# Convolution module of a flow-matching backbone: output, LayerNorm and residual in token order, mean and scale read from PSUM, relayout on two DMA queues

## The chip, the cores and the metric

The kernel runs on the 8 cores of one Trainium2 chip. All cores run the same program on different tokens and don't exchange data. The metric is the device time of the slowest core in microseconds; less is better.

## What is computed

One inference step of a backbone of four layers. Layers 0 and 2 mix tokens by neighbourhood attention, layers 1 and 3 by a convolution module; each is followed by a squared-ReLU MLP. The model width is 1024, and each core holds 1536 tokens. Only the convolution module changes:

```python
def conv_module(h, w_pw1, w_dw, b_dw, ln_g, ln_b, w_pw2):
    a, g = jnp.split(h @ w_pw1, 2, axis=-1)
    u = a * jax.nn.sigmoid(g)
    u = lax.conv_general_dilated(u, w_dw[:, None, :], window_strides=(1,),
        padding=[(15, 15)], dimension_numbers=('NWC', 'WIO', 'NWC'),
        feature_group_count=D_MODEL) + b_dw
    u = jax.nn.silu(layer_norm(u, ln_g, ln_b))
    return u @ w_pw2
# in the layer:  x = x + g1 * conv_module(modulate(rms_norm(x, norm_g), sh1, sc1), ...)
#                x = x + g2 * sq_relu_mlp(modulate(rms_norm(x, norm_g'), sh2, sc2), ...)
```

The convolution has 31 taps along the tokens and acts on each channel alone; the LayerNorm is over the 1024 channels of a token.

## The kernel before

Activations lie with channels on the partitions: 8 chunks of 128 channels by 1536 tokens, in 3 token tiles of 512 (`xT` is the f32 residual, `hT` the bf16 input of a product). The order of all work is written out by hand: a small class keeps one list per engine and puts a wait in front of an operation for each event that it needs, so each engine works its list in order. TensorE's writes go to 8 PSUM banks taken in turn; banks in `held` are left out of the turn. Weights come in 1 MB pieces by DMA on POOL's queue into a ring of three slots; `done_piece` queues the next piece, which waits until TensorE has left the slot. Small work is queued beside products: `defer` holds an operation back for some ticks, `bq` is a list of items, and `tick(n)`, called after each product, takes n of them.

`conv_layer` runs in this order:

- For each of 4 pieces of pw1 (`j`), for each token tile, four products; `pw1_evac` forms a x sigmoid(g) (ScalarE, VectorE) and writes bf16 with the tokens split by their remainder modulo 4: token = 4 tau + f, stored as f planes of tau.
- `relayout(j)` moves that piece into the convolution's layout with 16 DMAs between places in SBUF (4 channel groups q by 4 values of f), all on SP's queue.
- From the second piece on, each pw1 piece is followed by two convolution chunks of 128 channels (`conv_chunk`), and the last two (6 and 7) come after all pieces. Chunks 6 and 7 need `relayout(3)`, the last. A chunk has 4 outputs f; each is 32 matmuls into one bank of 384 columns (tau), at 4 places of the array at once. ScalarE evacuates each with the bias (L1245) into `vv`, ordered chunk, f, tau. After f = 1 and f = 3, VectorE casts the finished pair of planes to bf16 (L1253) and ScalarE squares it (L1256).
- `stats` sums channels and their squares with a matrix of ones (L1217) into banks SMB and SQB; that of chunk c stands in TensorE's list behind the first f of chunk c + 1.
- `build_w` makes a tap table (VectorE, L1198), four for each chunk; those of chunks 6 and 7 are made as soon as the chunks before have left the buffers.
- From the sums, 96 partitions wide, come mean and 1/std (L1323 to L1336). `ln_bcast(t)` spreads both over 128 partitions into two PSUM banks, and ScalarE copies them to SBUF (L1350, L1352).
- `ln_chunk(t, ch)` subtracts the mean and multiplies by the scale, two operations of 128x512 in f32 (L1366, L1370): chunks 2, 5 and 7 of every tile on POOL, the others on VectorE, each with two tiles of its own for the result. All read the SBUF copies. `ln_silu` (ScalarE, L1378) writes `hT`.
- pw2: for tile 0 the first four outputs are summed chunk by chunk while the silus arrive (L1398); then their gates, then the other products, each followed by `gate` (VectorE, L1413: residual plus gated product) and by the squares and sums of the next RMS norm (L575 on ScalarE, L582 on TensorE, L594 and L597 for its scale, L611 on VectorE, L632 on ScalarE). LayerNorm of tiles 1 and 2 and the norm of the tiles that are done are taken from `bq`, two items behind each product.

Since pw2's input is in the order f, tau, its output is so too, and `gate` reads and writes the residual, which is in token order, with a step of four elements. After `conv_layer` comes the MLP, whose products (L654) need the normed tile.

Of the kernel before, what the change touches and what calls it, by code (L numbers as in the profile page):

```python
# [347 lines left out]
def build_program():  # L348
# [763 lines left out]
    def conv_layer(l):  # L1112
# [4 lines left out]
        vv = vv.rearrange("p (c f t) -> p c f t", c=8, f=4)  # L1117
# [19 lines left out]
        for n in range(2):  # L1137
# [3 lines left out]
            up2.append((ap.rearrange("p (g w) -> p g w", g=8), parts, P.new_sem(f"cvs{l}_{n}")))  # L1141
# [29 lines left out]
        def relayout(j):  # L1171
# [11 lines left out]
            for q in range(4):  # L1183
                for f in range(4):
                    P.dma("sp", lambda e, q=q, f=f: e.dma_start(
                        out=dst[32 * f:32 * f + 32, q::4, :],
                        in_=u3[32 * q:32 * q + 32, :, f, :]),
                        dsem, reads=flat + halo, writes=[dst_r[q * 4 + f]])
# [21 lines left out]
        def stats(ch):  # L1210
            for half, bk in ((0, SMB), (1, SQB)):
                src = sqc[:, half * 1536:(half + 1) * 1536].rearrange("p (f t) -> p f t", f=4)

                def fn(e, src=src, bk=bk):
                    ins = None
                    for t in range(NT):
                        ins = e.matmul(ps[bk][32 * t:32 * t + 32, :],  # L1217
                                       lhsT=ones_b[:, 0:32], rhs=src[:, :, t * 128:(t + 1) * 128],
# [4 lines left out]
        def conv_chunk(ch):  # L1223
# [4 lines left out]
            for f in range(4):  # L1228
# [14 lines left out]
                if f == 0 and lag:  # L1243
                    stats(lag.pop(0))
                P.op("act", lambda e, f=f, pi=pi: e.activation(  # L1245
                    out=vv[:, ch, f, :], in_=ps[pi][:, 0:NTAU], func=AF.Identity,
                    bias=V("bdw", 1, i * 8 + ch)),
                    reads=[ps_r[pi], vecs_r], writes=[v_r[ch][f]])
                if f % 2 == 0:
                    continue  # L1250
                hf = f // 2
                o = hf * 768
                P.op("dve", lambda e, f=f, o=o: e.tensor_copy(  # L1253
                    out=sqc[:, o:o + 768].rearrange("p (f t) -> p f t", f=2), in_=vv[:, ch, f - 1:f + 1, :]),
                    reads=v_r[ch][f - 1:f + 1], writes=[sq_r[0][hf]])
                P.op("act", lambda e, f=f, o=o: e.activation(  # L1256
                    out=sqc[:, 1536 + o:2304 + o].rearrange("p (f t) -> p f t", f=2),
                    in_=vv[:, ch, f - 1:f + 1, :], func=AF.Square),
                    reads=v_r[ch][f - 1:f + 1], writes=[sq_r[1][hf]])
# [82 lines left out]
        def ln_bcast(t):  # L1342
            pm, pq = LB[t]
            for pb_, src, src_r in ((pm, mean, mean_r), (pq, rstd, rstd_r)):
# [6 lines left out]
                 reads=[ps_r[pm]], writes=[cm[1]])  # L1351
            P.op("act", lambda e: e.activation(out=cr[0][:, :], in_=ps[pq][:, :], func=AF.Copy),  # L1352
                 reads=[ps_r[pq]], writes=[cr[1]])

        def ln_chunk(t, ch):
            tc = slice(t * 128, (t + 1) * 128)
            (m_, m_r), (r_, r_r) = cpy[t % 2]
            if ch in (2, 5, 7):
# [187 lines left out]
```

How the kernel before makes its waits and increments, by code:

```python
                def body(e):  # L301
                    for it in eng.items:
                        if it[0] == "wait":
                            e.wait_ge(it[1].h, it[2])
                        else:
                            ins = it[1](e)
                            ins.then_inc(it[2].h, it[3])
```

## Time and profile before

| | us |
|---|---|
| median of 3 runs | 2704.92 |
| lowest and highest of them | 2704.63, 2833.44 |
| the profiled execution | 2705.91 |
| its span, slowest core (core 2) | 2704.4 |
| spans of the 8 cores | 2690.0 to 2704.4 |
| busy in that span: TensorE, VectorE, ScalarE, POOL | 2466.1, 1150.4, 1036.4, 299.1 |

The highest run was a disturbed one. The profile is of one execution on its slowest core; times of rows are in microseconds from the start of the span. PE is TensorE, DVE VectorE, ACT ScalarE; POOL and SP also issue DMAs. The convolution module of layer 1 lies between about 816 us and 1050 us, that of layer 3 between about 2117 us and 2350 us.

### The profile page before, as it was taken

The numbers are of one execution on the slowest core, as the hardware profiler recorded it, in microseconds if no ns is written. First come the engines' busy times: TensorE is split into PE (matmuls) and PEld (weight loads), VectorE is DVE, ScalarE is ACT, GpSimd is POOL, SyncE is SP. The second block draws the span as 40 slices with busy tenths as digits, with TensorE's granted clock in tenths as the row PEclk, the third lists the DMA queues.
The fourth block names the chain that finished last, engine by engine and source line by source line (L and its number), as shares of the span: only waits on it lengthen the run. The fifth ranks groups of instructions, "written<-read, shape, count | busy, mean of one in ns | idle before, by whom it ended". The sixth has DMA issues, their size and how long they took to land.

```text
span 2704.4 us, 41883 instructions; the slowest of 8 cores (2690.0 to 2704.4 us)
## 1 busy us (share of the span) xinstructions
PE 2466.1 (91%) x14955; PEld 1081.2 (40%) x15184; DVE 1150.4 (43%) x1552; ACT 1036.4 (38%) x1571; POOL 299.1 (11%) x323
## 2 busy tenths in 40 slices
PE   2888889999999978999999888899999997799998
PEld 1322224444444433444443222344444453344443
DVE  2344445323325665323244445453232656732333
ACT  4455555302224356302254555551031435630224
POOL 1122210000000030000002222000000002100000
PEclk8999979999999988999999999899999997899999
DMA  9754534555534202555448434155553331122322
GB/s 210 157 74 69 69 54 67 93 95 94 94 63 89 59 1 40 103 103 99 78 73 152 56 55 55 20 89 100 97 94 63 61 60 29 32 47 48 59 51 94
DMA packets 136506, 205.99 MB, mean 76 GB/s; under 512 B 73136, under 2 KB 83376, under 8 KB 135536
## 3 DMA queue, kind: packets, MB, share of 16 engines
q0 software_dynamic: 107824, 158.16, 38.0%
q1 hardware_dynamic: 28480, 45.14, 5.1%
q8 instruction: 126, 2.06, 0.3%
q14 instruction: 76, 0.62, 0.1%
HBM read 322.89 MB, written 31.46 MB: 131 GB/s over the span
## 4 chain that ended last, share of the span: by engine, by line
PE 77%; DVE 6%; issue 6%; ACT 5%; DMA 5%; SPq 0%; DVEq 0%; POOL 0%; ACTq 0%; POOLq 0%
PE pp L654 23%; PE ps L654 19%; PE pp L677 6%; PE ps L884 5%; PE pp L1271 3%; PE pp L1003 3%; PE ps L1028 3%; PE ps L677 2%; PE ps L1271 2%; PE pp L1398 2%; PE pp L1237 2%; DVE scr L976 2%; PE ps L582 2%; PE ps L1037 1%; ACT scr L1021 1%
## 5 line engine op out<-in xcount | busy, mean ns | idle before, releaser
L723 DVE TENSOR_TENSOR big<-big 128x512 bf16<-128x512 f32 x384 | 265.7, 692 | 414.5 <-ACT big L721 414.5
L654 PE MATMUL ps<-hTs,ring 128*128 128x512 bf16 x1488 | 338.4, 382 | 13.8 <-ACT hTs L632 8.8
L654 PE MATMUL pp<-hTs,ring 128*128 128x512 bf16 x1520 | 342.9, 380 | 1.9
L654 PE MATMUL pp<-big,ring 128*128 128x512 bf16 x1362 | 304.9, 379 | 2.7 <-ACT big L721 1.2
L419 POOL DMA_DIRECT2D ring<-wall x140 | 99.0, 707 | 1772.1 <-PE ps L654 512.1
L721 ACT ACTIVATE big<-ps 128x512 f32<-128x512 f32 x190 | 113.2, 596 | 471.9 <-PE ps L654 465.1
L575 ACT ACTIVATE scr<-xTs 128x512 bf16<-128x512 f32 x216 | 133.5, 627 | 336.0 <-DVE xTs L693 276.9
L693 DVE SCALAR_TENSOR_TENSOR xTs<-pp,mod,xTs 128x512 f32<-128x512 f32 x156 | 116.7, 750 | 330.6 <-PE pp L654 239.2
L976 DVE TENSOR_TENSOR scr<-pp,scr 128x768 f32<-128x768 f32 (+2 forms) x192 | 174.7, 911 | 141.9 <-PE pp L1009 70.1
L721 ACT ACTIVATE big<-pp 128x512 f32<-128x512 f32 x194 | 115.4, 596 | 296.1 <-PE pp L654 293.1
L884 PE MATMUL ps<-hTs,ring 128*128 128x512 bf16 x666 | 196.7, 390 | 31.3 <-DVE big L902 9.5
L654 PEld LDWEIGHTS ps<-hTs,ring 128*128 128x128 bf16 x1520 | 148.5, 98 | 192.1 <-issue 18.2
L1021 ACT ACTIVATE scr<-scr 128x768 bf16<-128x768 f32 (+2 forms) x192 | 154.9, 808 | 181.7 <-DVE scr L976 131.8
L654 PEld LDWEIGHTS pp<-hTs,ring 128*128 128x128 bf16 x1552 | 151.2, 98 | 181.6 <-issue 1.8
L654 PE MATMUL ps<-big,ring 128*128 128x512 bf16 x896 | 199.4, 379 | 1.4 <-ACT big L721 0.6
L654 PEld LDWEIGHTS pp<-big,ring 128*128 128x128 bf16 x1392 | 135.5, 98 | 162.4
L677 PE MATMUL pp<-big,ring 128*128 128x512 bf16 x815 | 191.0, 382 | 4.1 <-DMA ring<-wall 3.0
L632 ACT ACTIVATE hTs<-scr,mod,coef 128x512 bf16<-128x512 f32 x192 | 146.5, 802 | 44.1 <-DVE scr L611 44.1
L611 DVE TENSOR_TENSOR scr<-xTs,ps 128x512 f32<-128x512 f32 x200 | 127.9, 682 | 50.4 <-ACT ps L597 47.4
L1003 PE MATMUL pp<-big 64*128 64x512 bf16 (+7 forms) x640 | 112.8, 347 | 37.6 <-DVE scr L976 21.4
L693 DVE SCALAR_TENSOR_TENSOR xTs<-ps,mod,xTs 128x512 f32<-128x512 f32 x84 | 62.9, 750 | 193.1 <-PE ps L654 157.2
L654 PEld LDWEIGHTS ps<-big,ring 128*128 128x128 bf16 x912 | 88.8, 98 | 106.5
(117 smaller groups left out, 2704.1 us busy)
## 6 DMA issues: line engine op xcount, KB each, us to landing
ring<-wall POOLq DMA_DIRECT2D x140, 1024.0 KB, 10.8
vo<-big SPq DMA_DIRECT2D x48, 256.0 KB, 6.2
kTo<-big SPq DMA_DIRECT2D x48, 256.0 KB, 2.1
scr<-rpbp POOLq DMA_DIRECT2D x64, 128.0 KB, 3.5
scr<-big SPq DMA_DIRECT2D x128, 54.0 KB, 3.8
xTs<-xT SPq DMA_DIRECT2D x3, 2048.0 KB, 18.7
yT<-scr SPq DMA_DIRECT2D x24, 256.0 KB, 2.1
big<-ckT POOLq DMA_DIRECT2D x2, 512.0 KB, 8.9
```

Of the source, the lines that this page charges most:

```text
L575: P.op("act", lambda e: e.activation(out=sq[:, :], in_=xT[:, t, c, :], func=AF.Square), reads=[xT_r[c][t]], writes=[sq_r])
L632: P.op("act", lambda e: e.activation(out=hT[:, c, tsl], in_=ta[:, :], func=AF.Identity, scale=cf[:, k, c, s_:s_ + 1], bias=md[:, sh0 + c, ...
L654: ins = e.matmul(ps[pi][:, :], lhsT=w[:, kc, fc * fw:(fc + 1) * fw], rhs=src[:, kc, t * 512:(t + 1) * 512], start=(kc == 0), stop=(kc == n ...
L677: ins = e.matmul(ps[pi][:, :], lhsT=ring[s][:, kc * fw + fc * 128:kc * fw + fc * 128 + 128], rhs=src[:, kc, t * 512:(t + 1) * 512], start= ...
L693: P.op("dve", lambda e: e.scalar_tensor_tensor(out=xT[:, t, fch, :], in0=ps[pi][:, :], scalar=md[:, gate_chunk0 + fch, s:s + 1], in1=xT[:, ...
L721: P.op("act", lambda e: e.activation(out=ta[:, :], in_=ps[pi][:, :], func=AF.Relu), reads=[ps_r[pi]], writes=[ta_r])
L723: P.op("dve", lambda e: e.tensor_tensor(out=hid[:, hc, t * 512:(t + 1) * 512], in0=ta[:, :], in1=ta[:, :], op=ALU.mult), reads=[ta_r], wri ...
L884: ins = e.matmul(ps[pi][:, :], lhsT=ring[s][:, kc * 512 + fc * 128:kc * 512 + fc * 128 + 128], rhs=hT[:, kc, tsl], start=(kc == 0), stop=( ...
L976: P.op("dve", lambda e: e.tensor_tensor(out=z[:, :, 0:n], in0=ps2[pp][:, :, 0:n], in1=Tt[:, :, o0 * 64:o0 * 64 + n], op=ALU.add), reads=[p ...
L1003: ins = e.matmul(ps[2 * pp + par][:, 0:n], lhsT=b.lhs(64 * par), rhs=b.rhs(64 * par), start=True, stop=b.gate is None, skip_group_check=True)
L1021: P.op("act", lambda e: e.activation(out=pt[:, :, 0:n], in_=src[:, :, 0:n], func=AF.Exp), reads=src_r, writes=[pt_r])
L1271: ins = e.matmul(ps[pi][:, :], lhsT=ring[s][:, kc * 512 + fc * 128:kc * 512 + fc * 128 + 128], rhs=hT[:, kc, t * 512:(t + 1) * 512], start ...
```

## The change

- `vv` is ordered chunk, tau, f, that is, in token order, and so are the bf16 casts and squares, the LayerNorm, `hT`, the product of pw2 and the gate. The evacuation writes with a step of four f32 elements; the casts, squares, LayerNorm and gate read and write contiguously.
- In chunks 6 and 7 the evacuations of f = 1 and f = 3 move to VectorE.
- A half of the cast and of the square now covers 192 tau with all four f, so both halves come after the fourth evacuation.
- The 16 relayout DMAs: those of f = 0 and 1 stay on SP's queue, those of f = 2 and 3 go to POOL's; each half has a semaphore.
- `ln_chunk` on VectorE reads mean and scale from the PSUM banks; the copies stay for POOL. ScalarE's copies are entered as writers of the banks, so that VectorE follows them.
- POOL has chunks 2, 5, 7 in tile 0 as before, and 1, 3, 5, 7 in tiles 1 and 2.

```diff
-        vv = vv.rearrange("p (c f t) -> p c f t", c=8, f=4)
+        vv = vv.rearrange("p (c t f) -> p c t f", c=8, f=4)
+        vt = vv.rearrange("p c t f -> p c (t f)")
...
-                    P.dma("sp", lambda e, q=q, f=f: e.dma_start(
+                    P.dma("sp" if f < 2 else "pool", lambda e, q=q, f=f: e.dma_start(
                         out=dst[32 * f:32 * f + 32, q::4, :],
                         in_=u3[32 * q:32 * q + 32, :, f, :]),
-                        dsem, reads=flat + halo, writes=[dst_r[q * 4 + f]])
+                        dsem[f // 2], reads=flat + halo, writes=[dst_r[q * 4 + f]])
...
-                                       lhsT=ones_b[:, 0:32], rhs=src[:, :, t * 128:(t + 1) * 128],
+                                       lhsT=ones_b[:, 0:32], rhs=src[:, t * 512:(t + 1) * 512],
...
-                P.op("act", lambda e, f=f, pi=pi: e.activation(
-                    out=vv[:, ch, f, :], in_=ps[pi][:, 0:NTAU], func=AF.Identity,
-                    bias=V("bdw", 1, i * 8 + ch)),
-                    reads=[ps_r[pi], vecs_r], writes=[v_r[ch][f]])
-                if f % 2 == 0:
-                    continue
-                hf = f // 2
+                if ch >= 6 and f % 2 == 1:
+                    P.op("dve", lambda e, f=f, pi=pi: e.tensor_scalar(
+                        out=vv[:, ch, :, f], in0=ps[pi][:, 0:NTAU], scalar1=V("bdw", 1, i * 8 + ch),
+                        scalar2=None, op0=ALU.add),
+                        reads=[ps_r[pi], vecs_r], writes=[v_r[ch][f]])
+                else:
+                    P.op("act", lambda e, f=f, pi=pi: e.activation(
+                        out=vv[:, ch, :, f], in_=ps[pi][:, 0:NTAU], func=AF.Identity,
+                        bias=V("bdw", 1, i * 8 + ch)),
+                        reads=[ps_r[pi], vecs_r], writes=[v_r[ch][f]])
+            for hf in range(2):
                 o = hf * 768
...
+                P.op("dve", lambda e, o=o: e.tensor_copy(
+                    out=sqc[:, o:o + 768], in_=vt[:, ch, o:o + 768]),
+                    reads=v_r[ch], writes=[sq_r[0][hf]])
+                P.op("act", lambda e, o=o: e.activation(
+                    out=sqc[:, 1536 + o:2304 + o], in_=vt[:, ch, o:o + 768], func=AF.Square),
+                    reads=v_r[ch], writes=[sq_r[1][hf]])
...
-                 reads=[ps_r[pm]], writes=[cm[1]])
+                 reads=[ps_r[pm]], writes=[cm[1], ps_r[pm]])
...
-            tc = slice(t * 128, (t + 1) * 128)
-            (m_, m_r), (r_, r_r) = cpy[t % 2]
-            if ch in (2, 5, 7):
+            tc = slice(t * 512, (t + 1) * 512)
+            if ch in ((2, 5, 7) if t == 0 else (1, 3, 5, 7)):
                 ta, ta_r = tmpp[nl["p"] % 2]
                 nl["p"] += 1
+                (m_, m_r), (r_, r_r) = cpy[t % 2]
                 eng = "pool"
             else:
                 ta, ta_r = tmpd[nl["d"] % 2]
                 nl["d"] += 1
+                pm, pq = LB[t]
+                m_, m_r, r_, r_r = ps[pm], ps_r[pm], ps[pq], ps_r[pq]
                 eng = "dve"
             P.op(eng, lambda e: e.tensor_tensor(
-                out=ta[:, :].rearrange("p (f t) -> p f t", f=4), in0=vv[:, ch, :, tc],
-                in1=m_[:, :].rearrange("p (f t) -> p f t", f=4), op=ALU.subtract),
+                out=ta[:, :], in0=vt[:, ch, tc], in1=m_[:, :], op=ALU.subtract),
...
-            xv = xT[:, t, fch, :].rearrange("p (s w f) -> p f s w", s=2, f=4)
+            xv = xT[:, t, fch, :]
             P.op("dve", lambda e: e.scalar_tensor_tensor(
-                out=xv, in0=ps[pi][:, :].rearrange("p (f s w) -> p f s w", f=4, s=2),
+                out=xv, in0=ps[pi][:, :],
```

## Rows read from the trace of the kernel before

**Rows 1.** The page's chain that ended last: shares of the span by engine.
```profile
PE 77%; DVE 6%; issue 6%; ACT 5%; DMA 5%; SPq 0%; DVEq 0%; POOL 0%; ACTq 0%; POOLq 0%
```
**Rows 2.** Busy time by stretch in layer 1; columns as in the first line.
```profile
core 2: us, PE busy (x) PEld busy (x) DVE busy (x) ACT busy (x) POOL busy (x), PEclk, DMA share, GB/s
...
860.00:943.90 83.90, 78.67 (x1034) 42.53 (x1034) 49.48 (x54) 32.75 (x51) 2.11 (x3) 1.00 0.36 71
...
966.20:982.60 16.40, 12.07 (x34) 3.52 (x33) 13.07 (x11) 7.63 (x11) 10.05 (x7) 0.64 0.00 0
982.60:1000.60 18.00, 12.82 (x42) 4.92 (x43) 16.14 (x18) 10.72 (x16) 7.08 (x6) 0.81 0.00 1
1000.60:1027.60 27.00, 17.54 (x71) 7.33 (x72) 24.62 (x26) 20.04 (x30) 9.27 (x6) 0.90 0.00 0
1027.60:1049.90 22.30, 19.51 (x71) 8.20 (x74) 12.58 (x16) 14.12 (x21) 0.76 (x1) 0.81 0.27 48
```
**Rows 3.** The chain in order of time (start, us, what), both layers: the first MLP product.
```profile
1049.90 1.73 PE pp L654 x8
...
2350.27 1.73 PE pp L654 x8
```
**Rows 4.** Groups by line and shape, 800 to 1080 us: busy us, mean ns, idle before.
```profile
L1413 DVE SCALAR_TENSOR_TENSOR xTs<-pp,mod,xTs 128x512 f32<-128x512 f32 x24 | 27.4, 1159 | 9.9 <-PE pp L1398 9.9
L1378 ACT ACTIVATE hTs<-big,vecs_s 128x512 bf16<-128x512 f32 x24 | 18.6, 805 | 12.6 <-DVE big L1370 12.6
L1366 DVE TENSOR_TENSOR big<-big 128x512 f32<-128x512 f32 x15 | 16.3, 1087 | 5.6 <-ACT big L1350 4.2 <-ACT hTs L1378 1.3
L1256 ACT ACTIVATE big<-big 128x768 bf16<-128x768 f32 x16 | 13.5, 844 | 1.5
L1245 ACT ACTIVATE big<-pp,vecs_s 128x384 f32<-128x384 f32 x22 | 12.7, 579 | 19.9 <-PE pp L1237 19.6 <-issue 0.3
L1253 DVE CAST big<-big 128x768 bf16<-128x768 f32 x16 | 8.9, 559 | 34.2 <-ACT big L1245 34.2
```
**Rows 5.** Timeline of VectorE in LayerNorm and gates: start, us, line, operation, idle before.
```profile
968.50 1.75 DVE L1366 TENSOR_TENSOR big<-big 128x512 f32<-128x512 f32 x1
...
982.08 4.30 DVE L1413 SCALAR_TENSOR_TENSOR xTs<-pp,mod,xTs 128x512 f32<-128x512 f32 x4 [2.73 <-PE pp L1398]
...
988.35 0.69 DVE L1366 TENSOR_TENSOR big<-big 128x512 f32<-128x512 f32 x1
```
**Rows 6.** Timeline of POOL in the same stretch.
```profile
969.66 1.71 POOL L1366 TENSOR_TENSOR big<-big 128x512 f32<-128x512 f32 x1
...
981.60 1.28 POOL L1366 TENSOR_TENSOR big<-big 128x512 f32<-128x512 f32 x1 [4.99 <-ACT big L1350]
...
984.31 1.29 POOL L1366 TENSOR_TENSOR big<-big 128x512 f32<-128x512 f32 x1
```
**Rows 7.** Timeline of TensorE in layer 1: start, us, line, operation, idle before.
```profile
943.96 2.75 PE L1237 MATMUL pp<-scr 128*32 128x384 bf16 x32 [4.12 <-DMA scr<-big]
...
979.00 3.61 PE L1398 MATMUL pp<-hTs,ring 128*128 128x512 bf16 x16 [0.77 <-ACT hTs L1378]
...
1009.02 3.40 PE L1398 MATMUL pp<-hTs,ring 128*128 128x512 bf16 x8 [2.63 <-ACT scr L575]
...
1027.65 1.87 PE L1398 MATMUL pp<-hTs,ring 128*128 128x512 bf16 x4 [3.95 <-DVE scr L611]
```
**Rows 8.** The page's costliest groups: contiguous residual, and a product with a PSUM operand.
```profile
L693 DVE SCALAR_TENSOR_TENSOR xTs<-pp,mod,xTs 128x512 f32<-128x512 f32 x156 | 116.7, 750 | 330.6 <-PE pp L654 239.2
...
L611 DVE TENSOR_TENSOR scr<-xTs,ps 128x512 f32<-128x512 f32 x200 | 127.9, 682 | 50.4 <-ACT ps L597 47.4
```
**Rows 9.** Timelines of the SP and POOL queues: DMA issues, start and us.
```profile
929.99 12.46 SPq L1185 DMA_DIRECT2D scr<-big  x16
...
927.69 0.70 POOL L419 DMA_DIRECT2D ring<-wall  x1 [32.84 <-PE ps L1271]
...
93.90 0.85 POOL L812 DMA_DIRECT2D scr<-rpbp  x1
```
**Rows 10.** DMA issues, 927 to 944 and 93.8 to 95 us: KB each, us to landing.
```profile
ring<-wall POOLq DMA_DIRECT2D x1, 1024.0 KB, 10.1
scr<-big SPq DMA_DIRECT2D x16, 54.0 KB, 3.4
...
scr<-rpbp POOLq DMA_DIRECT2D x1, 128.0 KB, 13.1
```
**Rows 11.** Timeline of VectorE: the last two tap tables of chunk 7.
```profile
943.71 2.62 DVE L1198 TENSOR_TENSOR big<-cst_s,wr 128x1152 bf16<-128x1152 bf16 x2
```

More of the change, by code:

```diff
@@ L1140, in conv_layer @@
             scr.live.extend(parts)
-            up2.append((ap.rearrange("p (g w) -> p g w", g=8), parts, P.new_sem(f"cvs{l}_{n}")))
+            up2.append((ap.rearrange("p (g w) -> p g w", g=8), parts,
+                        [P.new_sem(f"cvs{l}_{n}_{k}") for k in range(2)]))
         NWT = 8
@@ L1211, in stats @@
             for half, bk in ((0, SMB), (1, SQB)):
-                src = sqc[:, half * 1536:(half + 1) * 1536].rearrange("p (f t) -> p f t", f=4)
+                src = sqc[:, half * 1536:(half + 1) * 1536]
                 def fn(e, src=src, bk=bk):
@@ L1244, in conv_chunk @@
                     stats(lag.pop(0))
-                P.op("act", lambda e, f=f, pi=pi: e.activation(
-                    out=vv[:, ch, f, :], in_=ps[pi][:, 0:NTAU], func=AF.Identity,
-                    bias=V("bdw", 1, i * 8 + ch)),
-                    reads=[ps_r[pi], vecs_r], writes=[v_r[ch][f]])
-                if f % 2 == 0:
-                    continue
-                hf = f // 2
-                o = hf * 768
[L1253 to L1259, printed above, removed]
+                if ch >= 6 and f % 2 == 1:
[9 more added lines that the diff above has]
+            for hf in range(2):
+                o = hf * 768
+                P.op("dve", lambda e, o=o: e.tensor_copy(
[4 more added lines that the diff above has]
+                    reads=v_r[ch], writes=[sq_r[1][hf]])
             lag.append(ch)
@@ L1350, in ln_bcast @@
             P.op("act", lambda e: e.activation(out=cm[0][:, :], in_=ps[pm][:, :], func=AF.Copy),
-                 reads=[ps_r[pm]], writes=[cm[1]])
+                 reads=[ps_r[pm]], writes=[cm[1], ps_r[pm]])
             P.op("act", lambda e: e.activation(out=cr[0][:, :], in_=ps[pq][:, :], func=AF.Copy),
-                 reads=[ps_r[pq]], writes=[cr[1]])
+                 reads=[ps_r[pq]], writes=[cr[1], ps_r[pq]])
         def ln_chunk(t, ch):
-            tc = slice(t * 128, (t + 1) * 128)
-            (m_, m_r), (r_, r_r) = cpy[t % 2]
-            if ch in (2, 5, 7):
+            tc = slice(t * 512, (t + 1) * 512)
+            if ch in ((2, 5, 7) if t == 0 else (1, 3, 5, 7)):
                 ta, ta_r = tmpp[nl["p"] % 2]
                 nl["p"] += 1
+                (m_, m_r), (r_, r_r) = cpy[t % 2]
                 eng = "pool"
```

## The prediction

> **What bounds the kernel now.** I read the page's chain first: TensorE holds 77% of it [rows 1], so time is won only where TensorE waits or runs slow. The change touches the two convolution layers alone. The busy time by stage shows where these lose it: in layer 1, the stretch from 860 us to 943.9 us, where pointwise products and convolution chunks alternate, keeps TensorE at 78.7 of 83.9 us at full clock. From 966.2 us (LayerNorm, pw2, residual) to 1049.9 us it is busy 61.9 of 83.7 us, at a granted clock of 0.64, 0.81, 0.90 and 0.81 of full speed [rows 2]; 0.5 would be the 1.2 GHz level throughout. The other convolution layer repeats this 1300.4 us later (the first MLP product after it: 1049.90 us and 2350.27 us [rows 3]), so I cost layer 1 and double it.
>
> Why does TensorE wait there? In the groups by line and shape VectorE's LayerNorm subtraction takes 1087 ns on average [rows 4]. The timelines show two populations: 1.75 us when POOL works beside it, 0.69 us alone [rows 5]; POOL takes 1.71 us there and 1.29 us beside VectorE's residual operation, which itself stays at 4.30/4 = 1.08 us [rows 5, 6]. So the LayerNorm operations of the two engines, both with two SBUF inputs, exclude each other; the residual operation, whose first input is in PSUM, doesn't block POOL. With VectorE late, TensorE sits in front of the silu outputs, the gates and the norm.
>
> A second wait is at 943.96 us: 4.12 us for the relayout DMAs, and then chunk 6's first 32 matmuls take 2.75 us [rows 7], the 1.2 GHz pace; half of it, 1.37 us, is the pace of one f at 2.4 GHz.
>
> **The change, part by part (us per convolution layer).**
>
> *Mean and scale from PSUM.* VectorE's operations have one SBUF input left, like the residual one, so I take them at 0.69 us: a 128x512 f32 product with a PSUM operand is 682 ns [rows 8]. No wait is gained: VectorE still waits for ScalarE's copy of the same bank. POOL's should fall to 1.29 us.
>
> LayerNorm of token tile 0, hand-scheduled from 966.2: VectorE has 5 chunks of 2 x 0.69 us and small gaps (done 973.4), POOL 3 of about 2.7 us (981.60 to 984.31 [rows 6]; done 974.6), and the last silu (0.8 us [rows 4]) ends at 975.4; before, the last sixteen matmuls waited for silus until 979.0 [rows 7]. The 32 pw2 matmuls that follow the silus need 32 x 0.216 = 6.9 us at full clock (sixteen took 3.61 us [rows 7]) and twice that at 1.2 GHz. The gates began at 982.1 [rows 5]. The first silu would end at 966.2 + 1.4 + 0.8 = 968.4; if the clock stays low, TensorE needs 968.4 + 13.8 = 982.2 and next to nothing is won (-0.4); if it rises as fast as at 943.96 (one 2.75 us batch at half pace [rows 7]), it ends at 976.3 (-6.3). The burst of 1009.02 was slow for longer, eight in 3.40 us [rows 7], so I take **-5.5**.
>
> *POOL half, tiles 1 and 2.* POOL has 4 x 2.7 = 10.8 us per tile, VectorE 4 x 1.4 + 8 gates. For tile 1 POOL would run from the ScalarE copies (about 976) to 987; its silu is needed when pw2 of tile 1 begins, about 991, so POOL stays hidden. If that cover went, each us of POOL would be a us of pw2.
>
> *Residual in token order.* The gate falls from 1159 ns [rows 4] to the contiguous form of the same operation, 750 ns [rows 8]: 24 x 0.41 = 9.8 us of VectorE. While pw2's second half of tile 0 runs (982.6 to 1000.6) four gates and three contended chunks lie in TensorE's way: **-2** of that stretch's 18.0 us. In tile 1 (1000.6 to 1027.6, 27.0 us) VectorE is busy 24.6 [rows 2]. After: 8 gates at 0.75, 3 chunks at 1.4 and 8 norm products at 0.69 = 15.7 us; TensorE needs 8 x (1.73 + 0.21) = 15.5; ScalarE is busy 20.0 [rows 2] and becomes the next to be late, its two table loads and the silus behind them holding the squares that TensorE waits for. So the stretch can't fall below about 20; I take 22: **-5**. Tile 2's stretch (22.3 us) waits for ScalarE's rstd with VectorE's norm products queued ahead of the gate; that stays, **-0.5**.
>
> *Token order of the convolution output.* ScalarE now writes 16 bytes apart, and no row of before shows such a write on ScalarE. Lower bound: the contiguous 579 ns [rows 4]. Upper bound from the same step on VectorE: (1159 - 750)/512 = 0.80 ns per element, times 384 = 0.31, so 0.88 us. I take 0.88, the only rows with this step being dear ones. The Trainium skill says the same in "Advanced Engine Details and Errata", Memory Cachelines: an access that changes its 16-byte line each time pays, and two hits are wanted; with this step there is one. By 0.58 instead, the sum would be 1.2 us per layer lower, 2676.5 us. No row here shows which holds for a write.
>
> *Cast and square after all four f.* Behind a chunk's last matmul there was one evacuation and one square (0.58 + 0.84 [rows 4]); now an evacuation and two squares: 0.88 + 1.69. The statistics matmuls stand in TensorE's queue behind the next chunk's first f, 1.37 us later, so a wait of about 1.0 us opens for chunks 0, 2, 4 and 6 (behind 1, 3 and 5 come other products or the relayout). Chunks 0 and 2 cost **+2.0**; 4 falls into the relayout's wait; 6 is counted next.
>
> *Relayout on two queues.* SP takes 12.46 us, to 942.4, to issue 16 DMAs [rows 9], so the last one issued decides. Eight take 6.2 us, to 936.2, plus 3.4 to land [rows 10]. POOL's eight cost about 0.85 us each [rows 9], issued by 936.8, in the queue behind the ring load of 927.69, which lands 10.1 us later, at 937.8 [rows 10]. All should be there at about 941, where TensorE now comes too: chunk 6 starts 2.8 earlier and skips the half-clock batch (-1.4). Against it: statistics of chunk 6 +1.35 (its last f waits on VectorE behind four tap-table builds, until 947; the last two took 2.62 us [rows 11]) and +0.8 at the end of chunk 7 (two squares behind a VectorE evacuation). Net **-2.0**. In the code POOL's relayout issues stand behind one ring load and before the next, 33 us later, so they delay no weights.
>
> Sum per layer: +2.0 - 2.0 - 5.5 - 2 - 5 - 0.5 = **-13.0**, twice -26. The profiled execution is 2705.9 us (span 2704.4), 1 us above the median of the runs, 2704.9; from the median: **2679 us**.
>
> **Rivals.**
>
> *The low clock stays* (0.20). TensorE starts each burst at 1.2 GHz; then tile 0 gives -0.4, tile 1 -3: -5.9 per layer, 2693 us. For it: the granted clock of 0.64 [rows 2]; after 3.95 us of pause at 1027.65 the next matmuls are slow again [rows 7].
>
> *POOL's relayout half lands late* (0.12). A DMA issued on POOL at 93.90, right behind a ring load, [rows 9] took 13.1 us to land [rows 10]. The last relayout DMA, issued about 936, would land at 949.1: chunk 6 8 us later than assumed and at half clock, +9.4 per layer: 2698 us. Against: its bytes are fewer (54 KB) and the ring load is nearly done by then.
> The Trainium skill, "SBUF — State Buffer", Who interferes with whom, adds that descriptors for POOL's DMAs can't be written while VectorE runs a two-port operation; the casts here (559 ns [rows 4]) may be such, which by two casts would make the sum 2681 us. No row shows it.
>
> *VectorE still excluded by POOL in spite of PSUM* (0.08), the change not doing what it says: only the gates win, -4 per layer, 2697 us. Against: the residual row [rows 5].
>
> *Strided evacuation very dear* (0.05), the other side: ScalarE falls behind TensorE's 1.37 us per f, and every statistics wait grows by the backlog and the write. At 2.0 us per evacuation the four waits are about 4.2 each and the tail 2.5 longer, 15 more than counted: +2 per layer, 2709 us. It decides from about 1.9 us, over three times the contiguous row; nothing here is that dear.
>
> *Everything fits* (0.05): the waits from 966 on nearly vanish, -24 per layer: 2657 us.
>
> **How the numbers follow.** The forecast has 0.50, with its own range 2668 to 2688 (tile 0 from -0.4 to -6.3, the evacuation 0.58 or 0.88, tile 1 2 us either way). The range 2662 to 2699 takes in the first three rivals. 2% is 54 us, about what a measurement of this kernel tells from no change; 27 us per layer is more than all of TensorE's idle time from 966 on (21.8) so faster by 2% has 0.02, slower 0.01.
>
> **What would show it.** Right: VectorE's and POOL's LayerNorm rows at 0.69 and 1.29 us with no 1.75 population; gates at 0.75; the gates of tile 0 beginning about 6 us nearer to the LayerNorm's start; SP issuing eight in about 6 us and no DMA wait over 1 us ahead of chunk 6; statistics waits of about 1 us; ScalarE's strided evacuation at 0.6 to 0.9 us. Wrong: 1.75 us rows remain, the evacuation is over 1 us, the granted clock from 966 on doesn't rise, or chunk 6 still waits for POOL's DMAs.

## The result and the profile after

The changed kernel takes **2671.02 us** (median of 4 runs), the kernel before, run beside it, 2706.77 us: ratio 0.9862, 95% interval 0.9846 to 0.9877, that is 35.75 us less by the medians. By the bound of 2% this counts as no change; the interval lies wholly below 1. The prediction was 2679 us (range 2662 to 2699). Runs far above the rest (3045 us here, others in the experiments) are disturbed ones and stand in no ratio and in no span below.

The first table is the map for all that follows. For every kernel the convolution module of a core was cut at the start of six events: first pw1 product, first convolution product, last convolution product, first LayerNorm operation on VectorE, first gate, last gate. The figures are medians over 8 cores and both layers, in us per layer; being medians, the stretches don't quite add up to the sum.

| kernel | before conv | conv products | to LayerNorm | to gate | gates | sum |
|---|---|---|---|---|---|---|
| before | 43.15 | 97.55 | 8.15 | 15.90 | 67.75 | 232.25 |
| after | 43.20 | 98.10 | 9.50 | 11.30 | 53.10 | 215.25 |
| e1 PSUM reads alone | 43.20 | 97.30 | 8.20 | 10.85 | 63.30 | 222.75 |
| e2 token order alone | 43.15 | 99.00 | 9.75 | 16.00 | 60.10 | 228.20 |
| e3 two queues alone | 43.20 | 92.95 | 8.60 | 15.90 | 66.80 | 227.30 |
| e4 after, statistics one f later | 43.20 | 92.25 | 9.40 | 10.85 | 51.90 | 207.85 |
| e5 after without PSUM reads | 43.15 | 98.00 | 9.55 | 15.90 | 57.90 | 224.55 |
| e6 after, POOL three chunks | 43.15 | 98.10 | 9.70 | 11.35 | 55.45 | 217.80 |
| e7 after, one queue | 43.15 | 99.00 | 9.50 | 10.95 | 51.90 | 214.60 |
| e9 e4, all evacuations on ScalarE | 43.15 | 92.45 | 9.75 | 11.20 | 52.70 | 209.50 |
| e10 e4, pauses filled | 43.15 | 92.50 | 9.40 | 10.85 | 51.15 | 207.25 |
| e11 e4, one queue | 43.20 | 96.95 | 9.40 | 11.90 | 53.40 | 214.85 |
| e12 e10, norm scale later | 43.50 | 92.10 | 9.40 | 11.15 | 49.20 | 206.05 |
| e13 after, contiguous write | 43.20 | 95.90 | 9.20 | 10.95 | 51.80 | 210.95 |

The change wins 17.0 per layer, and the rest of the program stands still within 2 us: ahead of layer 1's module 812.1 us before and 813.9 after, between the two modules 1069.0 and 1069.1, behind 354.2 and 354.4. Between the 16 modules of a kernel (8 cores by two layers) the gates differ by 1.4 to 3.2 us and the sums by 2.2 to 8.3, so differences below about 1.5 in these two columns decide nothing.

The table holds one execution of each kernel, and executions differ: the median core of the changed kernel took 2665.7 us in the one of the table, 2659.9 and 2660.8 in two others. Where it matters, a second figure is therefore given "by the spans": the span of the median core, averaged over a kernel's runs, compared between two kernels and halved, since the change touches two layers. By the spans the change wins 18.5 per layer.

Busy time by stretch of the changed kernel, core 2, layer 1; it answers to [rows 2]. The cuts are the first convolution product, about the end of chunk 6's first f, about the last statistics, the first LayerNorm operation, the first gate, the first product of tile 1, that of tile 2, and the first MLP product.

```profile
core 2: us, PE busy (x) PEld busy (x) DVE busy (x) ACT busy (x) POOL busy (x), PEclk, DMA share, GB/s
851.83:936.30 84.47, 80.67 (x1070) 43.67 (x1070) 45.72 (x50) 40.88 (x50) 15.47 (x27) 1.00 0.33 70
936.30:953.00 16.70, 12.12 (x255) 8.54 (x256) 11.25 (x14) 8.00 (x10) 0.00 (x0) 1.00 0.01 2
953.00:959.30 6.30, 4.47 (x10) 1.64 (x11) 0.69 (x2) 4.40 (x7) 0.00 (x0) 0.55 0.00 1
959.30:971.10 11.80, 10.95 (x35) 3.77 (x33) 6.54 (x11) 7.64 (x11) 9.23 (x8) 0.66 0.00 0
971.10:985.85 14.75, 12.42 (x45) 4.82 (x44) 9.91 (x15) 11.19 (x17) 8.78 (x8) 0.88 0.01 2
985.85:1007.06 21.21, 17.55 (x73) 7.39 (x72) 16.29 (x25) 19.01 (x28) 9.74 (x8) 0.92 0.00 0
1007.06:1024.30 17.24, 15.70 (x72) 6.93 (x73) 9.67 (x15) 12.91 (x20) 0.74 (x1) 1.00 0.36 62
```

From the LayerNorm's start to the MLP TensorE now needs 65.0 us instead of 83.7 [rows 2], and its idle time there fell from 21.8 to 8.4 (65.0 less the four busy times). VectorE's work of 66.4 us in that stretch [rows 2] became 42.4.

The groups by line and shape answer to [rows 4, 5, 6]: evacuation (L1253, on VectorE L1248), square (L1262), cast (L1259), gate (L1419), LayerNorm (L1373 and L1376).

```profile
L1253 ACT ACTIVATE big<-pp,vecs_s 128x384 f32<-128x384 f32 x19 | 18.7, 987 | 13.8 <-PE pp L1239 13.8
L1248 DVE TENSOR_SCALAR big<-pp,vecs_s 128x384 f32<-128x384 f32 x3 | 2.8, 933 | 4.6 <-PE pp L1239 4.6
L1262 ACT ACTIVATE big<-big 128x768 bf16<-128x768 f32 x16 | 12.6, 835 | 3.6 <-DVE big L1248 3.0
L1419 DVE SCALAR_TENSOR_TENSOR xTs<-pp,mod,xTs 128x512 f32<-128x512 f32 x24 | 17.6, 747 | 17.4 <-PE pp L1404 17.3
L1373 DVE TENSOR_TENSOR big<-big,ps 128x512 f32<-128x512 f32 x13 | 8.8, 679 | 3.7 <-ACT big L1355 3.7
L1376 DVE TENSOR_TENSOR big<-big,ps 128x512 f32<-128x512 f32 x13 | 8.9, 688 | 1.6 <-ACT scr L575 0.2 <-DVE big L1373 0.2 <-ACT big L1357 0.2
L1373 POOL TENSOR_TENSOR big<-big 128x512 f32<-128x512 f32 x11 | 14.0, 1271 | 41.4 <-PE ps L1350 31.3 <-ACT hTs L1384 6.6 <-ACT big L1355 3.5
```

VectorE's LayerNorm operations are at 0.68 us and POOL's at 1.27, and the two populations of [rows 5] are gone; the gate is at 0.75. The evacuation at 0.99 us is above the dearer of the two values assumed.

TensorE before the statistics of chunks 0, 2, 4, 5, 6 and 7, with the idle time in brackets, and behind them chunks 0 and 7 in the kernel before:

```profile
859.96 0.93 PE L1219 MATMUL ps<-big,onesb 128*32 128x512 bf16 x6 [1.05 <-DVE big L1259]
894.70 0.87 PE L1219 MATMUL ps<-big,onesb 128*32 128x512 bf16 x6 [1.11 <-DVE big L1259]
929.36 0.85 PE L1219 MATMUL ps<-big,onesb 128*32 128x512 bf16 x6 [1.12 <-DVE big L1259]
937.12 0.80 PE L1219 MATMUL ps<-big,onesb 128*32 128x512 bf16 x6 [0.96 <-DVE big L1259]
944.92 0.93 PE L1219 MATMUL ps<-big,onesb 128*32 128x512 bf16 x6 [1.22 <-DVE big L1259]
952.49 0.93 PE L1219 MATMUL ps<-big,onesb 128*32 128x512 bf16 x6 [2.29 <-DVE big L1259]
```

```profile
867.23 0.67 PE L1217 MATMUL ps<-big,onesb 128*32 128x512 bf16 x6 [0.17 <-DVE big L1253]
...
959.97 0.63 PE L1217 MATMUL ps<-big,onesb 128*32 128x512 bf16 x6 [1.57 <-DVE big L1253]
```

All six waits before are 0.17, 0.17, 0.18, none, 0.23 and 1.57. So the waits grew by 5.4 us per layer, and a wait stands where none was: behind chunk 5, which before had the relayout's wait of 4.12 us [rows 7].

The queues of SP and POOL, and their DMA issues from 919 to 945 us (KB each, us to landing), which answer to [rows 9, 10]:

```profile
923.46 6.38 SPq L1187 DMA_DIRECT2D scr<-big  x8
...
921.29 0.72 POOL L419 DMA_DIRECT2D ring<-wall  x1 [27.09 <-PE ps L1276]
923.95 4.44 POOL L1187 DMA_DIRECT2D scr<-big  x8 [1.95 <-DVE big L1181]
...
ring<-wall POOLq DMA_DIRECT2D x1, 1024.0 KB, 9.7
scr<-big SPq DMA_DIRECT2D x8, 54.0 KB, 6.0
scr<-big POOLq DMA_DIRECT2D x8, 54.0 KB, 5.7
```

All 16 are issued by 929.8, and here TensorE waits for none of them (in two of the 16 modules it waits over 1 us, 1.64 and 1.19); POOL's issue, 0.56 us each, is cheaper than the 0.85 assumed, and the ring load in front of them holds none back for long.

TensorE in tiles 1 and 2: the wait for the squares of tile 1, the product behind it, and in tile 2 the two waits that answer to 3.95 us at 1027.65 [rows 7] and 2.31 us at 1042.01 before, whose row stands last:

```profile
997.79 0.39 PE L582 MATMUL ps<-scr,onesb 128*128 128x512 bf16 x1 [2.28 <-ACT scr L575]
998.00 3.57 PE L1404 MATMUL pp<-hTs,ring 128*128 128x512 bf16 x8
...
1007.06 1.89 PE L1404 MATMUL pp<-hTs,ring 128*128 128x512 bf16 x8 [1.38 <-DVE scr L611]
...
1018.26 0.38 PE L582 MATMUL ps<-scr,onesb 128*128 128x512 bf16 x1 [1.54 <-ACT scr L575]
1018.48 1.89 PE L1404 MATMUL pp<-hTs,ring 128*128 128x512 bf16 x8
```

```profile
1042.01 0.38 PE L582 MATMUL ps<-scr,onesb 128*128 128x512 bf16 x1 [2.31 <-ACT scr L575]
```

Behind the pause of 2.28 us eight products take 3.57 us, the pace of the 1.2 GHz level; behind 1.38 and 1.54 they take 1.89, full pace. Tile 2 has no half-pace product any more, and its granted clock is 1.00 instead of 0.81.

### The profile page after: what moved, and what is told of

The parts are those of the page before. It is cut to its first block, busy times and chain, and to the rows that moved or that the text cites. A ratio compares the mean times of both kernels' runs of the same rounds, so it can differ in the third digit from the quotient of the medians.

```text
span 2668.6 us, 41955 instructions; the slowest of 8 cores (2657.3 to 2668.6 us)
## 1 busy us (share of the span) xinstructions
PE 2445.8 (92%) x14955; PEld 1077.7 (40%) x15184; DVE 1107.2 (41%) x1552; ACT 1051.0 (39%) x1563; POOL 336.8 (13%) x395
## 4 chain that ended last, share of the span: by engine, by line
PE 77%; DMA 6%; ACT 6%; issue 5%; DVE 5%; POOL 1%; DVEq 0%; ACTq 0%; POOLq 0%; SPq 0%
PE pp L654 23%; PE ps L654 19%; PE pp L677 7%; PE ps L884 4%; PE pp L1276 3%; DMA scr<-rpbp 3%; PE pp L1003 2%; PE ps L677 2%; PE pp L1404 2%; PE ps L1028 2%; PE ps L1276 2%; PE pp L1239 2%; PE ps L582 2%; DMA ring<-wall 2%; DVE scr L976 1%
## 5 line engine op out<-in xcount | busy, mean ns | idle before, releaser
L654 PEld LDWEIGHTS ps<-hTs,ring 128*128 128x128 bf16 x1520 | 148.6, 98 | 192.3 <-issue 18.7
L611 DVE TENSOR_TENSOR scr<-xTs,ps 128x512 f32<-128x512 f32 x200 | 127.9, 682 | 50.7 <-ACT ps L597 47.4
```

What stands on the lines that cost most here:

```text
L654: ins = e.matmul(ps[pi][:, :], lhsT=w[:, kc, fc * fw:(fc + 1) * fw], rhs=src[:, kc, t * 512:(t + 1) * 512], start=(kc == 0), stop=(kc == n ...
```

## The experiments

The theory after the result: the PSUM reads win most; token order wins at the gates and loses in the statistics; the two queues only make room that the statistics waits fill. Each part was run alone on the kernel before, then taken out of the changed one, then the suspected waits were removed.

**e1, PSUM reads alone.** The kernel before, with VectorE's LayerNorm reading the banks.

```diff
-                    reads=[ps_r[pm]], writes=[cm[1]])
+                    reads=[ps_r[pm]], writes=[cm[1], ps_r[pm]])
...
                 nl["d"] += 1
+                pm, pq = LB[t]
+                m_, m_r, r_, r_r = ps[pm], ps_r[pm], ps[pq], ps_r[pq]
```

> The kernel before, with one part of the change: VectorE's LayerNorm operations read mean and scale from the PSUM banks instead of the SBUF copies (POOL keeps chunks 2, 5, 7 and the copies). Theory A, that the exclusion between VectorE's and POOL's two-input operations was the largest single loss: the 1.75 us rows vanish (0.69 us on VectorE, 1.28 us on POOL), the stretch from the LayerNorm's start to the first MLP product falls from 83.5 us by about 10 us per convolution layer, and the time is about 2685 us. Theory B, that the strided gate was the larger loss and the LayerNorm had slack: about 4 us per layer, about 2697 us.

Ratio 0.9949 (0.993 to 0.9968). By the table it wins 9.5 per layer, as theory A has it; by the spans 6.9, and the time of 2694 us lies between the two theories. The groups show the operation itself:

```profile
L1368 DVE TENSOR_TENSOR big<-big,ps 128x512 f32<-128x512 f32 x15 | 10.2, 683 | 7.0 <-ACT big L1350 3.7 <-ACT hTs L1380 3.3
L1368 POOL TENSOR_TENSOR big<-big 128x512 f32<-128x512 f32 x9 | 11.5, 1275 | 50.7 <-PE ps L1345 38.2 <-ACT big L1350 7.2 <-ACT hTs L1380 5.3
L1415 DVE SCALAR_TENSOR_TENSOR xTs<-pp,mod,xTs 128x512 f32<-128x512 f32 x24 | 27.2, 1150 | 10.8 <-PE pp L1400 10.7
```

The LayerNorm rows are those of the changed kernel, with the old gate at 1.15 us. 5.05 of the 9.5 us lie before the first gate, 4.45 in the gates' stretch.

**e2, token order alone.** The change without PSUM reads, POOL's fourth chunk, the second queue and VectorE's evacuations.

```diff
...
-                if ch >= 6 and f % 2 == 1:
+                if False:
...
-            if ch in ((2, 5, 7) if t == 0 else (1, 3, 5, 7)):
+            if ch in (2, 5, 7):
...
```

> The kernel before, with token order alone: strided evacuation on ScalarE, cast and square after the fourth evacuation, contiguous LayerNorm and gate; no PSUM read, POOL chunks 2, 5, 7, relayout on one queue, no evacuation on VectorE. Theory A: the convolution stage grows by about 4 us per layer (waits of 1.1 us in front of the statistics and a longer end), the contiguous gate (0.75 us) gives back about 6 in the stretches after the LayerNorm: about -2 per layer, 2702 us. Theory B (the gate was the larger loss): -8 per layer, about 2690 us.

Ratio 0.9969 (0.9956 to 0.9982), 4.05 per layer: between the two theories. The table splits it: +3.05 in the convolution and its end, −7.65 at the gates. What it does to tile 2 is seen in TensorE's timeline, first e1 and then e2, the first product of tile 2 and the later wait for a square:

```profile
1005.88 2.59 PE L1400 MATMUL pp<-hTs,ring 128*128 128x512 bf16 x7 [2.09 <-DVE scr L611]
...
1019.52 0.38 PE L582 MATMUL ps<-scr,onesb 128*128 128x512 bf16 x1 [2.30 <-ACT scr L575]
1019.73 2.79 PE L1400 MATMUL pp<-hTs,ring 128*128 128x512 bf16 x8
```

```profile
1030.55 1.89 PE L1402 MATMUL pp<-hTs,ring 128*128 128x512 bf16 x7 [1.38 <-DVE scr L611]
...
1041.75 0.38 PE L582 MATMUL ps<-scr,onesb 128*128 128x512 bf16 x1 [1.54 <-ACT scr L575]
1041.97 1.89 PE L1402 MATMUL pp<-hTs,ring 128*128 128x512 bf16 x8
```

With the old gate (e1) tile 2 takes 21.4 us from its first product to the MLP's, with the new gate (e2) 17.2, as after the whole change. In this stretch VectorE does nothing but gates and products of the norm (L611), and only the gate differs. So the shorter gate alone wins tile 2: both pauses hang on VectorE's list, where the gate stands, and with them goes the slow pace behind them.

**e3, two queues alone.** The kernel before, with the relayout DMAs of f = 2 and 3 on POOL's queue.

```diff
-                    P.dma("sp", lambda e, q=q, f=f: e.dma_start(
+                    P.dma("sp" if f < 2 else "pool", lambda e, q=q, f=f: e.dma_start(
...
```

> The kernel before, with the relayout on two queues alone. Theory A: the wait of 4.1 us in front of chunk 6 goes, and with it the half-clock batch behind it (1.4 us); chunk 7 then waits up to 1 us for its tap tables: -4.5 per layer, about 2696 us. Theory B, that POOL's half lands late behind the ring load: the wait stays at 2 us or more, no change, about 2704 us.

Ratio 0.9969 (0.9957 to 0.998), 4.95 per layer, 4.6 of it in the convolution products: as theory A has it. TensorE's idle time before convolution products that waited for the relayout is 1.4 us in both layers of core 2 together, and 7.9 in the kernel before. The three parts alone add up to 18.5 per layer by the table, and 17.0 is won together; by the spans they add up to 16.2, and 18.5 is won together. So these sums don't tell whether the parts help or hinder each other; the runs that take a part out do.

**e5, the change without PSUM reads.** VectorE reads the copies again.

> The changed kernel, but VectorE's LayerNorm operations read mean and scale from the SBUF copies again; POOL keeps its four chunks in tiles 1 and 2. Theory A (exclusion is the largest loss): the rows of 1.7 us come back and the stretch from the first pw1 product to the last gate grows from 215.6 by 8 to 10 us per layer, about 2689 us. Theory B (with gates at 0.75 us VectorE has slack, so a blocked VectorE costs little): +3 per layer, about 2677 us.

Ratio 0.9925 (0.9903 to 0.9946); 9.3 per layer are lost (9.6 by the spans), as theory A has it and at least as much as e1 wins alone. The LayerNorm on VectorE is back at its old level or above it (1.16 us for the subtraction, 1.30 for the product; 1.09 before [rows 4]):

```profile
L1374 DVE TENSOR_TENSOR big<-big 128x512 f32<-128x512 f32 x13 | 16.9, 1300 | 1.6 <-DVE big L1371 0.3 <-ACT big L1357 0.2
L1371 POOL TENSOR_TENSOR big<-big 128x512 f32<-128x512 f32 x11 | 16.4, 1493 | 44.4 <-PE ps L1350 31.2 <-ACT big L1355 8.4 <-ACT hTs L1382 4.9
```

The mechanism of the forecast's largest term stands from both sides.

**e6, POOL's three chunks in every tile.**

```diff
-            if ch in ((2, 5, 7) if t == 0 else (1, 3, 5, 7)):
+            if ch in (2, 5, 7):
```

> The changed kernel with chunks 2, 5 and 7 on POOL in every tile, as before the change. Theory A: 1.4 us more VectorE work per tile lies beside products that ScalarE paces: 0 to +1.5 us per layer, 2671 to 2674 us. Theory B (the half on POOL carries part of the gain): +4 per layer, about 2679 us.

Ratio 0.9873 (0.9839 to 0.9907), 2.55 per layer more than after, 2.35 of it in the gates (3.2 by the spans): POOL's fourth chunk is worth about that, between the two theories. The intervals of the two ratios overlap, so its size is not settled. With it the gates' 14.65 us are nearly accounted for: 4.45 in e1, 7.65 in e2, 2.35 here.

**e7, the change with one queue.** All 16 relayout DMAs on SP again.

> The changed kernel with all 16 relayout DMAs on SP's queue. Alone on the kernel before, the two queues took 4.75 us off the stretch from the first pw1 product to the last gate. Theory A, that in the changed kernel this gain is mostly used up by new waits (statistics, tap tables, evacuations on VectorE): a DMA wait of 1 to 3 us returns in front of chunk 6 and the stretch grows by only 1 to 1.5 us per layer, about 2673 us. Theory B (the gains add): +4.7 per layer, about 2680 us.

Ratio 0.9851 (0.9825 to 0.9876): no loss shows, nor does one by the spans. The wait in front of chunk 6 is back, 2.1 to 3.7 us, a little more than theory A has, but the convolution products take only 0.9 longer; the gates take 1.2 less, which is within the spread between cores. The two queues, worth 4.95 us alone, are worth 0.9 in the convolution inside the change and nothing that shows in the time.

**e4, the change with the statistics one f later.** The wait of the statistics is covered by one more f of the next chunk.

```diff
-                if f == 0 and lag:
+                if f == 1 and lag:
```

> The changed kernel, with the statistics of chunk c moved in TensorE's list from behind the first f of chunk c + 1 to behind the second. Theory A: the idle time in front of the statistics (1.1 us each behind chunks 0, 2, 4 and 6) goes, since the second f gives 1.37 us more: -3.5 per layer, about 2664 us. Theory B: the time is set by ScalarE's evacuations and the tap tables of chunk 7, and the wait only moves: no change, about 2671 us.

Ratio 0.9846 (0.978 to 0.9911), runs of 2662.31 and 2670.55 us, too few to tell the time from the changed kernel's. The table does: 7.4 per layer less than after (5.5 by the spans), 5.85 of it in the convolution products, more than theory A has. Of the six waits only that behind chunk 7, 2.29 us, is left.

**e11, the same with one queue.**

> The statistics one f later, and the relayout on SP's queue alone. Theory A (the two queues were hidden behind the statistics waits: within the change they were worth nothing, since TensorE came late to chunk 6 anyway): with those waits gone TensorE comes to chunk 6 in time, and the one queue costs what it cost in the kernel before: the stretch of the convolution matmuls rises from 92.95 to about 97 us per layer, the time by about 8 us against the run with two queues. Theory B (the DMAs land in time on one queue as well, or the clock gives it back): less than 1.5 us per layer, under 3 in the time.

Ratio 0.9876 (0.9859 to 0.9893), 2675.38 us. It decides what e7 left open. TensorE's idle time before convolution products that waited for the relayout, both layers of core 2 (us, times), first e4 with one queue (this run), then e7, where one of the two waits ended last with a tap table (L1200):

```profile
  DMA scr<-big: 8.5, 2
```

```profile
  DVE scr L1200: 3.7, 1
  DMA scr<-big: 3.1, 1
```

In e4 itself no such wait is left on this core (in two of the 16 modules one is, 1.14 and 1.43 us); in most modules TensorE now waits 1.1 to 1.7 us for a tap table in front of chunk 6. Theory A holds: the convolution products take 96.95.

In that stretch, where both waits lie, the later statistics alone win 2.05 (e7 99.00, this run 96.95), the two queues alone 0.9 (e7 99.00, after 98.10), and both together 6.75 (e4 92.25). In the sum neither alone wins anything that shows (e7 214.60, this run 214.85, after 215.25), and both together win 6.75 per layer (e4 207.85), by the spans 5.4. Each of the two waits covers most of the other.

**e13, contiguous write.** The changed kernel with the evacuations written contiguously; the reordering of the tokens is left out.

```diff
...
-                        out=vv[:, ch, :, f], in_=ps[pi][:, 0:NTAU], func=AF.Identity,
+                        out=vt[:, ch, f * NTAU:(f + 1) * NTAU], in_=ps[pi][:, 0:NTAU], func=AF.Identity,
```

> The changed kernel with the convolution's evacuations written contiguously (place f of the chunk instead of every fourth element), everything else as it is. The order of the tokens is wrong then: the reordering is what is left out. This prices the 16-byte step by itself: the rows of ScalarE's evacuation should fall from 0.98 to 0.58 us. Theory A (the waits for the statistics are the two halves that now come after the fourth evacuation): each wait of about 1.3 us falls by the 0.4 us of one evacuation, four per layer, and the end of chunk 7 by 0.35: 2 us per layer, about 2667. Theory B (they are the dear write: four of 0.98 and two squares of 0.84 make 5.6 us per chunk, more than TensorE's 5.5, so ScalarE lags through the chunk): the waits nearly vanish, 4 to 5 us per layer, about 2661.

Lowest run 2665.3 us, 4.3 per layer less than after (2.2 by the spans): 2.2 in the convolution, 0.3 at its end, the rest behind it, within the spread. The evacuation, and the waits of chunks 0, 2 and 7:

```profile
L1253 ACT ACTIVATE big<-pp,vecs_s 128x384 f32<-128x384 f32 x19 | 11.0, 578 | 19.5 <-PE pp L1239 19.5
...
867.98 0.93 PE L1219 MATMUL ps<-big,onesb 128*32 128x512 bf16 x6 [0.64 <-DVE big L1259]
902.46 0.72 PE L1219 MATMUL ps<-big,onesb 128*32 128x512 bf16 x6 [0.86 <-DVE big L1259]
...
958.46 0.94 PE L1219 MATMUL ps<-big,onesb 128*32 128x512 bf16 x6 [2.02 <-DVE big L1259]
```

The six waits (0.64, 0.86, 0.74, 0.49, 0.67, 2.02) are 2.3 us shorter in all than after: theory A. Theory B counts a chunk too short: its f = 1 and f = 2 have 36 matmuls each, not 32, and the 136 of a chunk take TensorE about 5.8 us, so ScalarE with 5.6 keeps up. Of the 0.9 us by which a wait of about 1.1 exceeds that of the kernel before, the step in the write makes 0.4 and the two halves after the fourth evacuation 0.5.

**e9, e4 with all evacuations on ScalarE.**

> The statistics one f later (as in the run before of that name), and in chunks 6 and 7 all four evacuations on ScalarE. The question is what the move of two evacuations to VectorE is worth there. Theory A (about nothing): on ScalarE four evacuations of 0.98 and two squares of 0.84 us make 5.6 us per chunk against TensorE's 5.5, so ScalarE keeps pace, and the end of chunk 7 (evacuation, two squares) is as long as before; the stage from the first pw1 product to the last gate stays within 1 us per layer of 209.6. Theory B (the move carries the end of the stage): ScalarE enters chunk 7 with the squares of chunk 6 still to do, 1.7 us late, and the LayerNorm starts that much later: 2 us per layer, about 4 in the time. Theory C (the move costs): in the changed kernel the evacuation of f = 1 of chunk 6 stood on VectorE behind 5 us of tap tables; without it chunk 6 is up to 1 us faster.

Ratio 0.9838 (0.9818 to 0.9857), as e4's. Convolution +0.2, its end +0.35, the rest (1.1) within the spread: theory A, for the LayerNorm starts 0.55 us later and not the 1.7 of theory B. Up to there the move of two evacuations to VectorE is worth about half a microsecond; the whole difference, 1.65 by the table and 1.9 by the spans, is not settled.

**e10, e4 with pauses filled.** Products whose result nobody reads are put ahead of and behind the last statistics and before tile 0's gates.

```diff
...
+        fill(9, next_ps())
         stats(lag.pop(0))
+        fill(6, next_ps())
...
```

> The kernel with the statistics one f later (2662 us), and idle matmuls added that nobody reads: 9 in front of the last statistics, 6 behind them, 9 behind the first half of pw2 of tile 0, each stretch one in which TensorE waited. Theory A, that the low clock behind pauses is a cost of its own: the granted clock from the last convolution matmul to the gates rises from about 0.6 to near 1, the four-pass products that spread mean and scale (about 3.8 us for six) halve, and the gates of tile 0 begin 2 to 4 us earlier: 2654 to 2658 us. Theory B, that ScalarE, VectorE and POOL set the pace there: no change or the added matmuls cost up to 1 us each, 2662 to 2666 us.

Ratio 0.9800 (0.9769 to 0.9831), 2658.0 us: the fastest kernel of the study, below both given ones. But only 0.6 per layer separate it from e4. On core 2, layer 1, the granted clock from the last statistics to the first gate is 0.81 instead of 0.71, and the eight products that spread mean and scale take 3.85 us instead of 5.82; yet the time to the LayerNorm (9.40) and from there to the first gate (10.85) is the same. So theory B holds: TensorE doesn't set the pace there, and that the filling itself wins is not shown.

**e12, e10 with tile 0's norm scale later.**

```diff
-            norm_chunk(nctx, fch, t)
+            norm_chunk(nctx, fch, t, 6 if (t == 0 and fch == 7) else 3)
```

> On top of the run with filled pauses: the last sum of squares of token tile 0, and with it Ln and Exp of its norm, three products later, so that ScalarE meets no silu behind them and loads one function table less (1.28 us) in front of the squares of tile 1. Theory A: the pause of 2.28 us in front of those squares falls by 1.3, and the half-pace products behind it (3.06 and 2.23 us for eight) by about 1: 2 us per layer, about 2654. Theory B: the norm of tile 0 comes later, its VectorE products run into tile 2's gates and the first MLP product, and nothing is won or 1 to 3 us per layer lost: 2658 to 2664.

Ratio 0.9848 (0.983 to 0.9865), 2667.6 us: theory B. The gates' stretch is 1.95 shorter, but the stretch between the two modules, which begins with the MLP, takes 1072.5 us instead of 1068.7, and the one behind the second module 359.1 instead of 354.5. In layer 3's MLP TensorE waits for the late norm, first e10, then this run:

```profile
2318.34 2.72 PE L654 MATMUL ps<-hTs,ring 128*128 128x512 bf16 x8 [3.07 <-DVE scr L611]
```

```profile
2321.14 3.57 PE L654 MATMUL ps<-hTs,ring 128*128 128x512 bf16 x8 [4.79 <-DVE scr L611]
```

## Why the prediction was right, point by point

The forecast of −13.0 per layer became −17.0 (−18.5 by the spans), and 2671 us lies in the likeliest case's own range, 2668 to 2688. Core 2, layer 1, shows each term (us):

| step of the prediction | forecast | measured |
|---|---|---|
| statistics waits and relayout, up to the LayerNorm | 0.0 | +1.2 |
| LayerNorm of tile 0, until the gates | −5.5 | −4.1 |
| second half of tile 0 | −2 | −3.8 |
| tile 1 | −5 | −5.8 |
| tile 2 | −0.5 | −4.9 |
| sum | −13.0 | −17.3 |

The measured terms are rounded one by one. The errors of the first four cancel (+1.2, +1.4, −1.8, −0.8), which is luck; the whole miss is that of tile 2.

**Mean and scale from PSUM: right.** VectorE at 0.68 us was forecast at 0.69, POOL's 1.27 at 1.29; e1 and e5 bind both to the PSUM operand. Up to the gates it gave 4.1 instead of 5.5, because TensorE's 32 products of tile 0 ran in 9.72 us: between the 6.9 of full and the 13.8 of half pace, so more of them ran at half pace than forecast. The granted clock of that stretch, 0.66, is hardly above the 0.64 before.

**Residual in token order: right on the operation (0.75), too small on tile 2.** This is the step that was mis-sized: "that stays, **-0.5**" was said of the wait for ScalarE's scale, with VectorE's products ahead of the gate. It measured −4.9. The wait did not stay. Those products and the gates are one list, and with the gate 0.4 us shorter each of the two pauses fell (3.95 to 1.38 and 2.31 to 1.54), and the half-pace products behind them went too. Before, tile 2 lost 19.5 − 15.7 = 3.8 us of busy time to the slow pace [rows 2]. e2 has this gain without the PSUM reads, e1 has not.

**Cast and square after all four f: the wait was right, their number not.** About 1.0 us was forecast, 0.96 to 1.22 measured, 0.72 more at the end against 0.8. But chunk 5 was said to fall behind the relayout; with the relayout early its wait of 0.96 stands open. The bursts of statistics behind the waits are slower too, 0.80 to 0.93 us for six matmuls against 0.63 to 0.72 before (0.98 behind chunk 5, where the relayout's pause stood in front).

**Relayout on two queues: right on the DMAs, wrong on the balance.** They land in time, chunk 6 waits for none on this core, and the half-pace batch is gone. Yet e7 shows nearly the whole gain used up: with the statistics late, TensorE comes later and waits 2.1 to 3.7 us in front of chunk 6, where with the statistics out of the way (e11) it waits 3.9 to 5.2. The prediction counted the gain against the waits of chunks 4, 6 and 7 and came to −2.0; with chunk 5's wait and the slower bursts nothing remains. A reading to set right: the 33 us of the forecast lie in front of the ring load of [rows 9]; the next load behind POOL's relayout issues came 91 us later, so the conclusion that they delay no weights stands.

**Strided evacuation.** The upper value, 0.88, was chosen and 0.99 measured: the step taken from VectorE's gate costs more on ScalarE. By the Trainium skill, "Advanced Engine Details and Errata", Memory Cachelines, an access that changes its 16-byte line each time pays; e13 agrees, with 0.58 us without the step. No other step was run, so the length of the line is not shown.

**The rivals.** "The low clock stays" fell in tile 2 (granted clock 1.00 against 0.81). In tile 1 it fell by the time (−5.8 against its −3), though one burst behind a pause still ran at half pace and the granted clock, 0.92 against 0.90, hardly rose. In tile 0 the granted clock stayed (0.66 against 0.64), but the time fell by 4.1 and not by 0.4. "POOL's relayout half lands late" fell with 5.7 us to landing. "VectorE still excluded" fell with the 0.68 us. "Very dear" begins at 1.9 us; the row is 0.99. "Everything fits" needs −24 from 966 us on, and there the change wins 18.7 (83.7 to 65.0); e4 comes to −24.4 in all, but by another road, with 5.3 of it in the convolution products. The rule of the Trainium skill that descriptors for POOL's DMAs wait for VectorE's two-port operations ("SBUF — State Buffer", Who interferes with whom) was not tested: POOL issued its eight between 923.95 and 928.4, and VectorE did nothing from 923.3 to 928.2.

## What to carry to other kernels

Before counting a removed wait as a gain, ask which other wait lies beside it: here the relayout and the statistics covered each other, worth 0.9 and 2.05 us alone and 6.75 together. A shorter operation is worth more than its own time where TensorE comes back at half pace behind the pauses that it feeds; cost a pause with the products behind it. Work put off in one stage (e12) has to be followed into the next stage before it is called won.

## What the runs showed of the hardware

- A write with a step of 16 bytes costs 0.41 us more for 384 f32 elements on ScalarE (0.99 against 0.58), about 1.07 ns per element, and on VectorE about 0.32 us (0.933 in the changed kernel, 0.616 in e13), 0.8 ns per element, the value of the gate's step [rows 4, 8].
- Eight small DMAs on POOL's queue 2.7 us behind a 1 MB load landed 5.7 us after issue, and the 1 MB load took 9.7; the 13.1 us of [rows 10] did not recur.
- How dear a pause of TensorE is shows behind it: in the rows above eight products took 1.89 us behind pauses of 1.38 and 1.54, and 2.72 to 3.57 behind 2.28, 2.30, 3.07 and 4.79. The length of the pause doesn't decide it alone. In the kernel before, the products behind a pause of 2.83 us ran at full pace:

```profile
1017.20 0.38 PE L582 MATMUL ps<-scr,onesb 128*128 128x512 bf16 x1 [2.83 <-ACT scr L575]
1017.41 1.89 PE L1398 MATMUL pp<-hTs,ring 128*128 128x512 bf16 x8
```

- The same kernel takes the one course on one core and the other on the next. In the changed kernel TensorE pauses 2.33 us behind the first gates of tile 0 in all 16 modules; the eight products behind it took 1.89 us in seven of them, whose gates took 51.7 to 52.0, and 2.61 to 2.92 in nine, whose gates took 53.1 to 53.3. That is the spread of that column.
